# Two-block kernel on one core: modulation pieces taken out of the expert stages, and other instruction orders where stages meet

## The chip, the cores and the metric

One Trainium2 chip, one of its cores. The metric is the device time of one execution in microseconds; lower is better. The kernel was executed three times for the median, and once more under the profiler. Engines: TensorE (PE), VectorE (DVE), ScalarE (ACT), GpSimd (POOL) and SyncE (SP), which here only issues DMAs. Each engine works through its own list of instructions in order and waits on semaphores.

## The reference, cut to what matters

Batch 1, 256 tokens (two tiles of 128 rows), width 1024, everything float32.

```python
def first_block(x, ...):
    h = x
    for layer in range(2):
        h = h + hybrid_mixer(rms_norm(h, norm1_g[layer]), w_in[layer], ..., w_out[layer], lb)
        h = h + expert_choice_ffn(rms_norm(h, norm2_g[layer]), w_router[layer], w_gate[layer], w_up[layer], w_down[layer])
    return rms_norm(h, final_norm_g)

def expert_choice_ffn(xn, ...):            # 16 experts, 32 tokens each
    affinity = softmax(xn @ w_router)
    gate, idx = top_k(affinity.T, 32)      # each expert picks its tokens
    xe = xn[idx]
    ye = (silu(xe @ w_gate) * (xe @ w_up)) @ w_down * gate
    return scatter_add(ye, idx)

def second_block(x, c, ctx, c_ctx, ...):   # layer 0: pool mixer, layer 1: attention
    for i in range(2):
        sh1, sc1, gt1, sh2, sc2, gt2 = split(silu(c) @ w_ada[i] + b_ada[i], 6)
        csh1, ... = split(silu(c_ctx) @ w_ada[i] + b_ada[i], 6)
        x = x + gt1 * norm(mixer(modulate(norm(x), sh1, sc1)))
        x = x + gt2 * norm(mlp(modulate(norm(x), sh2, sc2)))
        # in layer 0 the same for ctx
```

The hybrid mixer projects to nine blocks of 512 columns, runs retention on four and HGRN2 on five, normalises both, multiplies by gates and applies w_out. The modulation vectors (w_ada: 2 layers x 1024 x 6144) depend on c alone, so they can be computed at any time before their use.

## The kernel before, in words

Time is a row of stages: layer 0 mixer, router, experts, layer 1 the same, then block 2 (pool mixer, MLP, attention, MLP). The context part of block 2 (its pool mixer and its MLP, nine pieces of weights in layer 0, nine in layer 1) is worked in between the experts.

**Weights and the ring.** All large weights come as pieces of 128 x 4096 float32 (2048 KB) into slots: four (0 to 3) of a ring of six, the last two of which (4, 5) hold w_high during mixers and MLPs, and two more (6, 7) in memory that the mixer has left. `item(name, slot, dmas)` writes down, at build time, in which slot a piece lies and how many pieces must be used before it may be loaded (`free_at`); PE counts used pieces in `weights_used`, and SP waits for that count ahead of each load (`load`, all loads at L2623). SP's list is in order, so a load that waits holds all behind it. Pieces of a mixer are sorted by `free_at`.

**Modulation pieces.** w_ada is cut into 12 pieces per layer. A piece is 8 matmuls (L537, 16 rows in a trace) into bank 6, ACT copies the row of 512 to `ada_s`, and four small matmuls (L552) turn it to columns, which PE can only do after ACT's copy. `ADA_EARLY`: six pieces per layer run in the mixer, between its projections. `ADA_LATE`: six per layer, one right after the output projection (`late_ada`), one after the logits, two after expert 0 and two after expert 1 (`LATE_AFTER`). `ada_bias` adds b_ada on DVE, `gains` makes the gains of the modulated norms.

**Split weights.** Mixer products are three passes over fp32r parts (L525, L526, L527): ACT copies a piece to w_high (`high_item`), DVE subtracts to get w_low (`low_item`). The activations are split likewise: `high_chunks` on ACT and `split_chunks` on DVE each write for every second bank a full xT and an xs_high (8 instructions each), and DVE subtracts both to xT_low (4 instructions).

**End of the mixer.** Order on ACT: last modulation row, `high_item(OUT_1)`, squares of the ret and hgrn outputs, sqrt of both (a table load ahead). On DVE: `low_item(OUT_0)`, sums, `low_item(OUT_1)`, then the hgrn rows (times 1/std), then gate x 1/std x ret rows, `ada_bias("early")`, `split_chunks`. PE: ret_out, hgrn_out, columns, transposes (L500), the output projection.

**Output projection and router.** Four products of 24 matmuls, tile 0 then tile 1, in banks 0 to 3; DVE adds each to h. Then a modulation piece, normalised rows xs of both tiles, 16 transposes, evacuation to xT with the gain, the logits of both tiles in one bank (L788), maximum, exp, affinity, a transpose of it (L796), four rounds of top-8 on DVE, spread (L802), gather (L815), expert 0 (L851 gate and up, L886 down).

**Block 2.** Attention's q, k, v weights are `mix2` items 0 to 2, w_o items 3 and 4, in a ring of four. PE: `turn_tile(0)` (L1211), projections (L1194), transposes of q (L1232) and k (L1239), scores (L1249).

ACT holds one set of function tables at a time; the program's first use of a function from another set is preceded by ACT_TABLE_LOAD.

## Time and profile before

| | us |
|---|---|
| median of 3 runs | 2110.59 |
| lowest, highest | 2109.51, 2112.42 |
| profiled execution, device time | 2113.23 |
| its span, first to last instruction | 2110.9 |
| PE busy in the span | 1744.7 (83%) |
| DVE, ACT, POOL busy | 796.9, 520.8, 36.4 |
| bytes by DMA | 629.10 MB, mean 298 GB/s |

All times of instructions are counted from the span's start. Busy shares are averages over stages of different kinds; the forty slices and the windows separate them. An instruction's row gives its start, how long it (or the merged group) took, engine, line, operation, output and inputs, and in brackets the engine's idle time before it and what ended it. Where a helper issues an instruction the line is the helper's (L425).

### The profile page before, as it was taken

To read this page: it belongs to the slowest core of one execution; us is meant where nothing else is said; L and a number is where in the kernel's file an instruction comes from. 1 tells how busy PE (TensorE), PEld (TensorE's weight loads), DVE (VectorE), ACT (ScalarE), POOL (GpSimd) and SP (SyncE) were. 2 spreads that over 40 slices of the span, in tenths; PEclk is the share of its full clock that TensorE was granted. 3 is DMA by queue.
4 is the path that set the end of the run, shared out by engine and by line. 5 is a ranking of instruction groups with operands and counts; after the bars stand their busy time and mean duration, and the time that the engine had idled before them with its cause. 6 is when DMAs were issued, how large, how long until landed. Compare 5 with 4: busy or idle time off the path is not lost.

```text
span 2110.9 us, 25989 instructions
## 1 busy us (share of the span) xinstructions
PE 1744.7 (83%) x10876; PEld 1150.9 (55%) x10876; DVE 796.9 (38%) x1175; ACT 520.8 (25%) x778; POOL 36.4 (2%) x42
## 2 busy tenths in 40 slices
PE   6998767678898849997677898866778999998998
PEld 5876423343454328875334354432247996457887
DVE  6594301211111026764201111121046676555766
ACT  5633110200000025432010000011144343343433
POOL 0000000000000000000000000000010000000000
PEclk9999778889999979998788999997889999998999
DMA  7475699999999993574899999999963454304451
GB/s 268 157 265 201 264 421 421 429 423 423 424 421 424 425 405 136 204 267 195 344 420 423 423 425 422 424 425 421 427 233 146 168 191 159 120 1 159 173 186 60
DMA packets 124799, 629.10 MB, mean 298 GB/s; under 512 B 5024, under 2 KB 7200, under 8 KB 99744
## 3 DMA queue, kind: packets, MB, share of 16 engines
q1 hardware_dynamic: 122000, 616.58, 72.9%
q0 software_dynamic: 2272, 9.44, 1.1%
q8 instruction: 73, 1.20, 0.2%
q10 hardware_dynamic: 432, 1.70, 0.2%
q14 instruction: 22, 0.18, 0.0%
HBM read 624.56 MB, written 3.15 MB: 297 GB/s over the span
## 4 chain that ended last, share of the span: by engine, by line
PE 57%; DMA 32%; DVE 5%; ACT 4%; issue 1%; SPq 0%; POOL 0%; DVEq 0%; ACTq 0%
DMA ring<-in_w_up 18%; PE bank L525 9%; PE bank L527 9%; PE bank L526 9%; PE bank L851 7%; DMA ring<-in_w_mlp_in 6%; PE bank L981 5%; PE bank L999 4%; DMA ring<-in_w_mlp_out 4%; PE bank L1194 2%; PE bank L537 2%; DMA ring<-in_w_in 1%; DVE w_low L425 1%; PE bank L1294 1%; ACT w_high L425 1%
## 5 line engine op out<-in xcount | busy, mean ns | idle before, releaser
L851 PE MATMUL bank<-ring,xeT 128*32 128x512 f32 x1984 | 285.2, 724 | 131.8 <-DMA ring<-in_w_up 131.5
L851 PEld LDWEIGHTS bank<-ring,xeT 128*32 128x32 f32 x1984 | 73.1, 124 | 333.1 <-issue 333.0
L425 ACT ACTIVATE silu_g<-bank 128x256 f32<-128x256 f32 x32 | 12.3, 384 | 741.7 <-PE bank L851 741.7
L425 DVE TENSOR_TENSOR hid_e<-silu_g,bank 128x256 f32<-128x256 f32 x32 | 13.5, 421 | 411.7 <-ACT silu_g L425 411.7
L525 PE MATMUL bank<-x_high,w_high 128*128 128x256 f32 x512 | 147.5, 288 | 11.0 <-DVE x_low L425 5.9
L2308 DVE TENSOR_TENSOR w_low<-ring,w_high 128x1024 fp32r<-128x1024 f32 x128 | 151.9, 1219 | 9.3 <-POOL y L425 4.9
L886 PE MATMUL bank<-ring,hid_T 128*32 128x256 f32 x2048 | 124.9, 390 | 29.9 <-DMA ring<-in_w_down 23.6
L981 PE MATMUL bank<-ctx_xT,ring 128*128 128x256 f32 x512 | 128.1, 417 | 25.7 <-DMA ring<-in_w_mlp_in 25.7
L1657 ACT ACTIVATE w_high<-ring 128x1024 fp32r<-128x1024 f32 x128 | 128.0, 1050 | 86.0 <-PE bank L527 86.0
L527 PE MATMUL bank<-x_high,w_low 128*128 128x256 f32 x512 | 146.4, 286 | 0.0
L526 PE MATMUL bank<-x_low,w_high 128*128 128x256 f32 x512 | 146.3, 286 | 0.0
L999 PE MATMUL bank<-ring,ctx_hid 128*128 128x512 f32 x256 | 122.4, 640 | 23.9 <-DMA ring<-in_w_mlp_out 23.9
L981 PEld LDWEIGHTS bank<-ctx_xT,ring 128*128 128x128 f32 x512 | 107.6, 212 | 47.7 <-DMA ring<-in_w_mlp_in 30.4
L525 PE MATMUL bank<-w_high,xs_high 128*128 128x512 f32 x256 | 106.9, 418 | 18.4 <-DVE xT_low L425 14.9
L425 DVE TENSOR_TENSOR w_low<-ring,w_high 128x2048 fp32r<-128x2048 f32 x44 | 100.8, 2292 | 25.1 <-ACT w_high L425 20.6
L886 PEld LDWEIGHTS bank<-ring,hid_T 128*32 128x32 f32 x2048 | 62.1, 111 | 82.6 <-DMA ring<-in_w_down 33.5
L525 PEld LDWEIGHTS bank<-x_high,w_high 128*128 128x128 f32 x512 | 98.6, 192 | 11.8 <-issue 11.6
L526 PE MATMUL bank<-w_low,xs_high 128*128 128x512 f32 x256 | 104.3, 407 | 0.0
L527 PE MATMUL bank<-w_high,xT_low 128*128 128x512 f32 x256 | 104.0, 406 | 0.0
L999 PEld LDWEIGHTS bank<-ring,ctx_hid 128*128 128x128 f32 x256 | 51.9, 206 | 91.6 <-issue 63.8
L527 PE MATMUL bank<-w_high,hid_low 128*128 128x512 f32 x256 | 101.5, 396 | 0.0
L525 PE MATMUL bank<-w_high,hid_high 128*128 128x512 f32 x256 | 101.5, 396 | 0.0
(275 smaller groups left out, 2630.9 us busy)
## 6 DMA issues: line engine op xcount, KB each, us to landing
ring<-in_w_down SPq DMA_DIRECT2D x64, 2048.0 KB, 25.5
ring<-in_w_gate SPq DMA_DIRECT2D x62, 2048.0 KB, 20.1
ring<-in_w_up SPq DMA_DIRECT2D x62, 2048.0 KB, 22.9
ring<-in_w_ada SPq DMA_DIRECT2D x24, 2048.0 KB, 9.9
ring<-in_w_mlp_in SPq DMA_DIRECT2D x24, 2048.0 KB, 8.6
ring<-in_w_mlp_out SPq DMA_DIRECT2D x24, 2048.0 KB, 7.9
ring<-in_w_in SPq DMA_DIRECT2D x18, 2048.0 KB, 9.1
ring<-in_w_out SPq DMA_DIRECT2D x4, 2048.0 KB, 8.1
```

The costliest lines, as they stand in the source:

```text
L425: self.ins, self.mine = op(*args, **kw), "none"
L525: mm(ps, lh, rh, start=first, stop=False, skip_group_check=True)
L526: mm(ps, lh, rl, start=False, stop=False, skip_group_check=True)
L527: return mm(ps, ll, rh, start=False, stop=last, skip_group_check=True)
L537: ins = mm(ps[32 * g:32 * g + 32, :], cT[:, 2 * g + k, :], w[:, 2 * g + k, :], start=k == 0, stop=k == 1)
L851: ins = mm(ps[32 * j:32 * j + 32, :], xeT[:, g % 2, c, i * CAP:(i + 1) * CAP], w[:, :, k, j, :, :], start=c == 0, stop=c == KC - 1, skip_g ...
L886: ins = mm(banks[q // 2][rows_, at_:at_ + 256], hidT[:, j, 32 * block:32 * block + 32], w[:, c, 256 * q:256 * (q + 1)], start=(n, c) == (0 ...
L981: ins = mm(ps[:, (j % 2) * S:(j % 2 + 1) * S], w[:, c, j * P:(j + 1) * P], cxT[:, c, :], start=c == 0, stop=c == KC - 1)
L999: ins = mm(ps[:, :], chid[:, c, t * P:(t + 1) * P], w[:, c, half * 512:(half + 1) * 512], start=c == 0, stop=c == 3)
L1194: ins = mm(ps[:, :], xT2[:, c, t * P:(t + 1) * P], w[:, c, :], start=c == 0, stop=c == KC - 1)
L1657: raw(w_high[:, n % 2, quarter(q)], ring[:, slot, quarter(q)], ACT.Copy).then_inc(S_("w_high_ready"), 1)
L2308: nc.vector.tensor_tensor(w_low[:, slot, quarter(q)], ring[:, slot, quarter(q)], w_high[:, n % 2, quarter(q)].bitcast(F32), ALU.subtract). ...
```

## The change

Three sorts of edits, in words:

1. Modulation pieces. The tables `EARLY_AFTER`, `ADA_LATE`, `LATE_AFTER`, `MOE_SLOTS` go. `ADA_EARLY` (six per mixer, at the same places), `ADA_REST` (four per layer, at the mixer's end and in the router) and `ADA_LAST` (four in block 2's attention) take their place; layer 1's mixer computes the last two pieces of layer 0 first. None is left among the experts. The slots of expert pieces rotate over 6, 7 once and then 4, 5, c, a, b, d.
2. The joints. Mixer end: squares and roots ahead of `high_item(OUT_1)`, `low_item(OUT_1)` behind `split_chunks`, sqrt tables loaded early by a one-column activation (`root_table`), ret rows multiplied by the gate first and by 1/std in place later; xs_high written by ACT from the banks for all chunks, xT_low made by DVE in one instruction from the bank. Router: h itself is transposed, 1/rms goes in as the scale of the exp; transposes and logits of tile 0 run inside the products of tile 1; banks 0 and 1 are used twice.
3. The start of a mixer: the first piece comes in two halves with their own semaphore, constants other than the identity and the masks are issued by SP behind it.

The diff, cut to its core (the signature changes of helpers are left out):

```diff
+ADA_EARLY = (pieces(0, 0, 6), pieces(0, 10, 12) + pieces(1, 0, 4))
+ADA_REST = (pieces(0, 6, 10), pieces(1, 4, 6) + pieces(1, 10, 12))
+ADA_LAST = pieces(1, 6, 10)
-LATE_AFTER = [{0: late[2:4], 1: late[4:6]} for late in ADA_LATE]
-MOE_SLOTS = (6, 7, 4, 5, 0, 1, 2, 3)
...
+        for piece, slot in zip(ADA_REST[layer], (b, d)):
+            item(("ada", *piece), slot, 1)
         for n in range(2):
             item(("w_out", layer, n), (c, a)[n], 1)
         count[2][4:6] = [count[0]] * 2
-        for n, slot in zip(ADA_LATE[layer][0:2], (b, d)):
-            item(("late", layer, n), slot, 1)
-        slots = itertools.chain(MOE_SLOTS, itertools.cycle(MOE_SLOTS[2:]))
+        for piece, slot in zip(ADA_REST[layer][2:], (b, d)):
+            item(("ada", *piece), slot, 1)
+        slots = itertools.chain((6, 7), itertools.cycle((4, 5, c, a, b, d)))
```

PE, end of the mixer, output projection and router:

```diff
             ret_out()
+            early_columns(len(ADA_EARLY[l]) - 1)
             hgrn_out()
-            early_columns(ADA_EARLY[l][-1])
             transposes(("mix", l), lambda t: xs[:, t, :], mix_ready)
+            rest_ada(0)
...
+            amid = {(0, 1): lambda: turn_rows(0), (1, 1): lambda: logits(0)}
             for t in range(NT):
                 for n in range(2):
...
                         fill(ins, name)
-            late_ada(ADA_LATE[l][0])
-            transposes(("x2", l), lambda t: xs[:, t, :], xs_ready)
+                        rest_columns(n)
+                        if n == 0:
+                            rest_ada(1)
+            turn_rows(1)
+            rest_ada(2)
+            logits(1)
+            rest_columns(2)
             pe.wait_ge(S_("affinity_ready"), NT * (l + 1))
...
+            rest_ada(3)
+            rest_columns(3)
```

PE, block 2:

```diff
+        ada_item(ADA_LAST[0], 1)
         turn_tile(0)
...
+                if (t, n) == (0, 0):
+                    last_columns(0, 1)
...
+        ada_item(ADA_LAST[1], 6)
         pe.wait_ge(S_("q_rot_ready"), NT)
...
+        last_columns(1, 6)
+        ada_item(ADA_LAST[2], 5)
         pe.wait_ge(S_("k_rot_ready"), NT)
...
+        last_columns(2, 5)
+        ada_item(ADA_LAST[3], 6)
...
         scores(1)
+        last_columns(3, 6)
```

ACT:

```diff
+                if (j, half) == (0, 0):
+                    act.wait_ge(S_("first_landed"), 16 * (l + 1))
...
-        act.dma_start(ident_all[:, :], consts).then_inc(S_("consts"), 16)
-        act.dma_start(AD[:, :, :].rearrange("p a b -> p (a b)")[:, 0:len(LEVELS) * P],
-                      masks).then_inc(S_("masks"), 16)
+        act.dma_start(ident_all[:, 0:P], consts[:, 0:P]).then_inc(S_("consts"), 16)
...
-                ins = f(logit[:, t, :], ps[:, t * NEXP:(t + 1) * NEXP], ACT.Exp,
-                        bias=rstats[:, t, 1:2], accum_out=rstats[:, t, 2:3])
...
+                free(f(logit[:, t, :], ps[:, 0:NEXP], ACT.Exp, scale=rinv[:, t:t + 1],
...
+                if e == NEXP - 1:
+                    root_table()
```

DVE:

```diff
+                    ins = stt(xT_low[:, c, :].rearrange("p (t n) -> p t n", t=NT),
+                              ps[:, at_:at_ + S].rearrange("p (t n) -> p t n", t=NT), gain(c),
+                              xs_high[:, :, c, :].bitcast(F32), ALU.mult, ALU.subtract)
...
             split_chunks(("mix", l), mix_gain)
+            low_item(OUT_1)
```

SP:

```diff
+                if name == ("mix", l, 0):
+                    sp.dma_start(whole[:, 0:4, :], halves[0]).then_inc(S_("first_landed"), 16)
+                    sp.dma_start(whole[:, 4:8, :], halves[1]).then_inc(landed[items[name][0]], 16)
+                if name == ("mix", 0, 0):
+                    sp.dma_start(ident_all[:, P:], consts[:, P:]).then_inc(S_("tables"), 16)
...
+                        if (e, n) == (0, 1):
+                            for piece in ADA_REST[l][2:]:
+                                early(("ada", *piece))
```

SP's list around expert 0 of layer 0, before. `ring_extra` are slots 6 and 7, a gate and an up row are the two halves of one half of an expert's gate and up weights.

```order
L2623 DMA ring_extra<-in_w_gate 128x4096
L2623 DMA ring_extra<-in_w_up 128x4096
L2623 DMA ring<-in_w_gate 128x4096
L2623 DMA ring<-in_w_up 128x4096
L2623 DMA ring<-in_w_down 128x4096 x2
L2623 DMA ring<-in_w_ada 128x8x512 x2
L2623 DMA ring<-in_w_gate 128x4096
L2623 DMA ring<-in_w_up 128x4096
L2623 DMA ring<-in_w_gate 128x4096
L2623 DMA ring<-in_w_up 128x4096
L2623 DMA ring<-in_w_down 128x4096 x2
L2623 DMA ring<-in_w_ada 128x8x512 x2
```

And of the change, from the same place:

```order
L2706 DMA ring_extra<-in_w_gate 128x4096
L2706 DMA ring_extra<-in_w_up 128x4096
L2706 DMA ring<-in_w_ada 128x8x512 x2
L2706 DMA ring<-in_w_gate 128x4096
L2706 DMA ring<-in_w_up 128x4096
L2706 DMA ring<-in_w_down 128x4096 x2
L2706 DMA ring<-in_w_gate 128x4096
L2706 DMA ring<-in_w_up 128x4096
L2706 DMA ring<-in_w_gate 128x4096
L2706 DMA ring<-in_w_up 128x4096
L2706 DMA ring<-in_w_down 128x4096 x2
```

The two pieces that stood behind expert 0 stand ahead of its ring loads, and the two behind expert 1 are gone.

PE's list from the last product of the output projection to the spread, layer 0, before:

```order
L527 MATMUL bank<-w_high,xT_low 128x512
L537 MATMUL bank<-ring,silu_c 32x512 x8
L500 MATMUL bank<-consts_sb,xs 128x128 x16
L788 MATMUL bank<-router_sb,xT 128x16 x16
L552 MATMUL bank<-consts_sb,ada_rows 128x2 x4
L537 MATMUL bank<-ring,silu_c 32x512 x8
L796 MATMUL bank<-consts_sb,affinity 16x128 x2
L802 MATMUL bank<-spread,ones 128x512 x2
```

And of the change:

```order
L528 MATMUL bank<-w_high,xT_low 128x512
L777 MATMUL bank<-consts_sb,h 128x128 x8
L539 MATMUL bank<-ring,silu_c 32x512 x8
L790 MATMUL bank<-router_sb,xT 128x16 x8
L554 MATMUL bank<-consts_sb,ada_rows 128x2 x4
L819 MATMUL bank<-consts_sb,affinity 16x128 x2
L539 MATMUL bank<-ring,silu_c 32x512 x8
L554 MATMUL bank<-consts_sb,ada_rows 128x2 x4
L827 MATMUL bank<-spread,ones 128x512 x2
```

Half of the transposes and logits have moved ahead into the projection, the transposes read h, and the second modulation piece stands behind the transpose of the affinity.

ACT's list at the end of layer 0's mixer, before:

```order
L425 ACTIVATE hgrn_off<-bank 128x512 x2
L425 ACTIVATE ada_rows<-bank 128x512
L425 ACTIVATE w_high<-ring 128x2048 x2
L425 ACTIVATE square<-bank 128x512 x2
L425 ACTIVATE xs,ssq<-bank 128x512 x2
L425 ACT_TABLE_LOAD
```

And of the change:

```order
L434 ACTIVATE hgrn_off<-bank 128x512 x2
L434 ACT_TABLE_LOAD
L434 ACTIVATE spare<-eps 128x1
L434 ACTIVATE ada_rows<-bank 128x512
L434 ACTIVATE square<-bank 128x512 x2
L434 ACTIVATE kdec,ssq<-bank 128x512
L434 ACTIVATE std<-ssq,eps 128x1
L434 ACTIVATE ret_stat<-ret_stat,eps 128x8
L434 ACTIVATE kdec,ssq<-bank 128x512
L434 ACTIVATE std<-ssq,eps 128x1
L434 ACTIVATE w_high<-ring 128x2048 x2
```

The table load stands ahead of the squares, and the conversion of the piece (w_high) behind both roots.

## Rows read from the trace of the kernel before

**Rows 1.** The page's part 2: GB/s in 40 equal slices of the span.

```profile
GB/s 268 157 265 201 264 421 421 429 423 423 424 421 424 425 405 136 204 267 195 344 420 423 423 425 422 424 425 421 427 233 146 168 191 159 120 1 159 173 186 60
```

**Rows 2.** Windows: us; busy PE, PEld, DVE, ACT, POOL; clock, DMA, GB/s.

```profile
300.00:500.00 200.00, 139.16 (x1071) 70.22 (x1070) 28.13 (x46) 29.02 (x49) 2.64 (x3) 0.86 1.01 424
...
1070.00:1300.00 230.00, 185.29 (x1228) 98.60 (x1232) 27.58 (x46) 16.81 (x31) 0.00 (x0) 0.90 1.01 424
```

**Rows 3.** Timeline of SP: loads around expert 0 and expert 1, layer 0.

```profile
219.75 16.72 SPq L2623 DMA_DIRECT2D ring<-in_w_ada  x2
262.01 0.34 SPq L2623 DMA_DIRECT2D ring<-in_w_gate  x1
...
284.20 8.69 SPq L2623 DMA_DIRECT2D ring<-in_w_ada  x2
```

**Rows 4.** Timeline, layer 0: end of the mixer, output projection, router, expert 0.

```profile
169.00 0.95 PE L552 MATMUL bank<-consts_sb,ada_rows 128*128 128x2 f32 x8
...
169.88 1.92 PE L537 MATMUL bank<-ring,silu_c 128*32 128x512 f32 x16
...
178.74 4.69 DVE L425 TENSOR_TENSOR w_low<-ring,w_high 128x2048 fp32r<-128x2048 f32 x2
...
179.89 1.28 ACT L425 ACT_TABLE_LOAD   x1
...
187.72 1.54 PE L500 MATMUL bank<-consts_sb,xs 128*128 128x128 f32 x6 [7.78 <-DVE xs L425]
...
193.57 0.47 PE L525 MATMUL bank<-w_high,xs_high 128*128 128x512 f32 x1 [1.96 <-issue]
...
217.86 0.69 DVE L425 TENSOR_TENSOR h<-h,bank 128x512 f32<-128x512 f32 x1 [4.93 <-PE bank L527]
...
232.78 3.25 PE L537 MATMUL bank<-ring,silu_c 128*32 128x512 f32 x16
...
236.38 0.41 DVE L425 COPY affinityT<-bank 16x256 f32<-16x256 f32 x1 [2.35 <-PE bank L796]
...
254.42 3.89 PE L851 MATMUL bank<-ring_extra,xeT 128*32 128x512 f32 x32 [0.94 <-issue]
```

**Rows 5.** A window at the mixer's end, layer 0, columns as in rows 2.

```profile
185.00:188.00 3.00, 0.28 (x2) 0.29 (x3) 2.58 (x5) 0.00 (x0) 0.00 (x0) 0.50 1.04 440
```

**Rows 6.** Timeline, layer 1: last sum, logits, first product of expert 0.

```profile
987.12 0.69 DVE L425 TENSOR_TENSOR h<-h,bank 128x512 f32<-128x512 f32 x1 [4.93 <-PE bank L527]
...
993.91 4.46 PE L788 MATMUL bank<-router_sb,xT 128*128 128x16 f32 x32 [2.02 <-ACT xT L425]
...
1022.22 2.04 PE L851 MATMUL bank<-ring_extra,xeT 128*32 128x512 f32 x16 [0.94 <-issue]
```

**Rows 7.** Timeline: the start of the program.

```profile
15.58 3.85 ACT L425 ACTIVATE w_high<-ring 128x2048 fp32r<-128x2048 f32 x2 [3.37 <-DMA ring<-in_w_in]
...
22.77 0.80 PE L525 MATMUL bank<-w_high,xs_high 128*128 128x512 f32 x1 [7.28 <-DVE xT_low L425]
...
28.84 0.50 PE L525 MATMUL bank<-w_high,xs_high 128*128 128x512 f32 x1 [0.97 <-DVE xT_low L425]
```

**Rows 8.** Timeline: the start of layer 1's mixer.

```profile
780.52 1.28 ACT L425 ACT_TABLE_LOAD   x1
781.82 0.29 ACT L425 ACTIVATE std<-ssq,eps 128x1 f32<-128x1 f32 x1
...
791.71 0.76 PE L525 MATMUL bank<-w_high,xs_high 128*128 128x512 f32 x1 [5.25 <-DVE xT_low L425]
...
797.73 0.51 PE L525 MATMUL bank<-w_high,xs_high 128*128 128x512 f32 x1 [1.35 <-DVE xT_low L425]
```

**Rows 9.** Timeline of PE in block 2: first transposes, q transposes, first scores.

```profile
1778.61 1.06 PE L1211 MATMUL bank<-consts_sb,xs 128*128 128x128 f32 x8 [2.00 <-issue]
...
1827.74 1.97 PE L1232 MATMUL bank<-consts_sb,q_rot 128*128 128x128 f32 x16 [1.94 <-DVE q_rot L425]
...
1832.85 3.65 PE L1249 MATMUL bank<-kT,qT 128*128 128x512 f32 x4 [0.98 <-DVE kT L425]
```

409 lines of the change are left out of this document (227 added, 182 removed).

## Prediction, made before the change was run

> **What bounds the kernel now.** I read the page's forty slices first, then the windows, and only then the order of time at the places where one stage meets the next. The reader is to see two kinds of stretch [rows 1]: long runs of slices at 420 to 429 GB/s, and slices at 136 to 268 GB/s. The first are the two expert stages, the others the mixers and block 2. The windows say it sharper [rows 2]: over 200 us in layer 0 and 230 us in layer 1 the DMA engines are busy at a share of 1.01 and move 424 GB/s, while PE is busy 139 of 200 us and 185 of 230 us. There a piece of weights (2048 KB = 2.097 MB) costs 2.097/0.424 = 4.95 us, whoever uses it, and no engine's work costs anything as long as slots come free in time. Between these stages the DMA has nothing to do for long, and what counts is the chain PE, ACT, DVE at each joint: mixer to output projection, output projection to router to expert 0, last expert to next stage.
>
> **1. Pieces out of the saturated stretch.** Before, a layer loads four modulation pieces in its expert stage. Two are issued at 219.75, ahead of the stretch, and two at 284.20, in it; the saturated stretch begins at 262.01, when expert 0 has used its second pair and expert 1's first load goes out [rows 3]. After, the two later ones are gone, and the slots in which the two earlier ones lay are free by the router, so that expert 1's first two pieces load there, in the gap ahead of the stretch. So four pieces fewer are left when the stretch begins: 4 x 4.95 = 19.8 us, twice: **39.6 us**. Condition: these two loads, in SP's order behind the four of expert 0, are in by the restart. Six pieces take 29.7 us from the end of the output projection, and the restart comes some 34 us after it (part 2), so yes, with 4 us to spare. The later pieces are used in block 2, where the DMA idles. Bounds: 19.8 us in all if the two preloads never come early, 41 if the stretch's other traffic shrinks with it.
>
> **2. Router joint, layer 0.** Now [rows 4]: the last hgrn output leaves PE by 180; ACT has converted w_out 1 ahead of the squares, a table load stands at 179.89, DVE converts for 4.69 us from 178.74, and only then come the normalised rows; PE transposes at 187.72 after 7.78 us of idle, and multiplies from 193.57. After, both conversions come behind the statistics, the sqrt table is loaded early, the ret rows are multiplied before the sqrt is known, and high and low parts are made without a full copy (8 instructions each on ACT and DVE in place of 8 on ACT and 12 on DVE, about 0.5 us each). Step by step with the same durations: hgrn output 179.9 (columns now ahead of it, +0.9), last rows 183.4, transposes to 184.5, first low part 187.1. But PE has modulation piece 0 to run there: 1.92 us at the full clock, 3.25 at the half [rows 4]. After the idle the granted clock is 0.50 of 2.4 GHz, that is 1.2 GHz [rows 5], and 2.6 us of idle remain; I take the low clock, and PE is ready at 188.8, **4.8 us** earlier (bounds 3 and 6.5).
>
> Into the output projection go, all on PE and on the path: two sets of columns (0.95 each), a piece (1.92), eight transposes (about 1.1, half of the sixteen at a joint) and the logits of tile 0 (half of 4.46 [rows 6], a bit less at full clock: 1.8), in sum **+6.7 us**. The other side: from the last sum at 217.86 to the copy of the affinities at 236.38 it is 18.5 us now, through normalise, transposes, the logits of both tiles, table load, exp, and a PE that runs a piece of 3.25 us at 232.78 ahead of the transpose which is on the path [rows 4]. After, per step: sum 0.7, eight transposes to 1.9, ACT statistics and four evacuations to 4.3 (a piece on PE hides in it), logits of one tile to 6.4, maximum and exp to 7.5, affinity to 8.4, copy at 8.65: **-10.0 us** (bounds 8 and 11). The search of the top 32 and the gather are as before, and the last piece with its columns (1.92 + 0.95, or some 5 at the low clock) lies beside the 6.9 us of the search; its cover would have to shrink by 2 us before it cost anything. Net 4.8 - 6.7 + 10.0 = **8 us** (bounds 4 and 11). The first expert started at 254.42, now about 246.4.
>
> **3. Router joint, layer 1.** The same, but from 987.12 to expert 0 at 1022.22 it is 35.1 us, not the 36.6 of layer 0 [rows 4, 6]: 1.5 us less to win, and the earlier half I put 0.5 lower. **6 us** (bounds 3 and 9).
>
> **4. The start.** PE's first product is at 22.77, behind the conversion at 15.58, which waited for its weights [rows 7]; by then x, weights, constants, masks and columns have come, 4.85 MB by their shapes, 12.1 us at 0.4 MB/us and 3.4 us for the rest. After, constants and masks stand behind the weights: x, 1.25 MB with columns and identity, by about 6 (3.1 + 3.4 is 6.5; ACT began at 6.6 before), the second half of the weights, 3.3 MB, at 11.7. Then two statistics without table loads 3.2, to 9.2; two conversions of 1.93, the second from 11.7, to 13.6; high parts 1.0, low parts 1.1: 15.8. That is 7.0, and the 0.97 us that PE waited at 28.84 for the next low part go too: **8 us** (bounds 2, if only copies and table loads go, and 9.5). The next item's weights land about 21 and are wanted by PE at 29.5.
>
> **5. Layer 1's start.** A table load (1.28) at 780.52, then a short wait for the weights, PE's first product at 791.71, and a stall of 1.35 us at 797.73 [rows 8]. After, the first piece takes the slot that expert 15's first pair frees, one piece earlier in SP's order; ACT may convert from 782.8, high and low to 788.8: 2.8 us, and the stall goes: **4.1 us** (bounds 1.3 and 4.1). The table load ahead of block 2 goes too, **1.3 us**.
>
> Here a rule speaks for more. What the row shows: the load takes 1.28 us and std begins at 781.82, at its end [rows 8]. The Trainium skill (ScalarE: Activation LUTs, What ACT_TABLE_LOAD costs) puts a drain of about 1.38 us behind each switch, 2.66 us in all. Eight switches leave the path (two at the start, two in each router joint, one ahead of layer 1's mixer, one ahead of block 2). By the page the sum would be 11 us larger, by the row it stands.
>
> **6. Block 2 pays.** Four pieces and four sets of columns come to PE's order. Piece 0 fits the 2.00 us ahead of 1778.61; its columns wait for ACT's copy: +1.4 in a stretch where PE is busy throughout. Piece 1 (1.92) fits the 1.94 us ahead of 1827.74. Pieces 2 and 3 stand between the q transposes and the scores at 1832.85, where PE idled 2.5 us and two times 2.87 come, with two waits for ACT's copy of the row behind its four copies of q: scores +3.35; the last columns +0.5; the four scores took 3.65 us at the low clock and gain 1 [rows 9]. In sum **+4 us** (bounds 0 and 8). Who waits: DVE's and ACT's softmax, directly. The kv weights are now issued when the MLP ends, alone on the queue, 4.95 us of bytes and wanted some 14 us later. The output weights load later too, about 40 us before use.
>
> **Sum.** 39.6 + 8 + 6 + 8 + 4.1 + 1.3 - 4 = 63 us. The profiled execution took 2113.23 with a span of 2110.9; it would take 2050.2, span 2047.9. The median of the runs is 2110.59, 2.64 under the profiled one: 2110.6 - 63 = **2047.6 us**.
>
> **Rivals.**
> *A, the sum as it stands:* 2047.6, own range 2037 to 2058.
> *B, the preload fails:* expert 1's pieces are held by pieces 2 and 3 of the modulation (PE reaches the last at about 10 us after the output projection; held past the restart it would be two pieces a layer). For: SP works in order. Against: 4 us to spare. 2047.6 + 19.8 = 2067.
> *C, joints gain little:* the clock stays at 1.2 GHz through the output projection, and the start is bound by its bytes. Router joints 3 us each worse, start 6 (its lower bound), block 2 at its upper bound 4: 16, that is 2064.
> *D, joints gain more:* PE's filled gaps hold 2.4 GHz through the joints, the gather too (matmuls that now run at the low clock): 3 for each of two gathers, 2.5 each for the output projections, 1 for block 2: 12, so 2036.
> *E, slower:* the ring. A load waits until all items but the last few are used. In the item tables of the code 12 expert-stage loads are issued with four or fewer pieces between them and the last release that they need; after the change it is 25, and two have three. If each of the 25 left the DMA idle for more than 63/25 = 2.5 us, nothing would be left; at a full piece, 4.95 us each, it is 2047.6 + 124 = 2171. Against it: the 12 of now show no slice below 420 GB/s in the stage [rows 1], and three pieces are 15 us of queue.
> *F, dearer table loads:* each load that is gone had held ACT as long again as its row shows (1.28 us); eight times that is 10 us more, 2037. Against it: at 781.82 the next instruction begins at the load's end. This mechanism is the one of the Trainium skill above.
> That the change does nothing of the kind I exclude: SP's rows show no modulation load behind expert 0.
>
> **Chances.** A 0.55, C 0.18, D 0.13, B 0.10, F 0.02, E 0.02. The likeliest is A: 2047.6. For eight in ten I reach to D and F below, 2034, and past C to 2065; B and E stay outside, and some of the tails. Same means within 0.2%, about what runs of this kernel tell from no change (their own spread is 0.14%): faster 0.97, same 0.01, slower 0.02, the last from E.
>
> **What would show it.** (1) The expert stages stay at 424 GB/s and are 19.8 us shorter from the first DMA of the stretch to the last expert's product; an idle of some us at a share under 1 within them is E. (2) From the last sum of the output projection to expert 0: 26.7 us. If it is over 30, the piece ahead of the logits or the last columns are on the path. (3) First product at about 15 us; at 20 the bytes bound it. (4) Two expert 1 loads land before the restart; else B. (5) The scores begin 4 to 5 us later, counted from the MLP's end. The prediction is wrong above all if (1) fails, which holds two thirds of it.

## The result and the profile after

| | before | after |
|---|---|---|
| median, us | 2110.05 (4 runs) | 2031.20 (4 runs) |
| lowest, highest | 2104.61, 2112.42 | 2030.25, 2033.38 |
| span of the profiled execution | 2110.9 | 2029.1 |

The ratio is 0.9631, 95% interval 0.9611 to 0.9651: 79 us faster. The forecast was 63 (2047.6, range 2034 to 2065), so the direction was right and the size too small, and 2031.2 lies 3 us under the range. Between the two spans there are 81.8 us; the profiled execution of before (2113.23) was 3.2 us above the median of this table.

Page of after, part 2, GB/s in 40 slices. The saturated runs are at the rate of [rows 1]; a slice is 50.7 us now and was 52.8.

```profile
GB/s 303 170 247 290 376 428 423 428 420 424 422 425 419 427 312 166 242 290 284 414 422 425 422 423 420 424 427 423 415 134 171 202 169 162 249 34 133 203 169 62
```

Both traces, cut at the same instructions (starts of TensorE's first products, ends of VectorE's last sums), beside what the prediction's terms give for each piece:

| from, to | before | after | gain | forecast |
|---|---|---|---|---|
| start, first product | 22.77 | 15.82 | 7.0 | 7.0 |
| to the last sum of the output projection, layer 0 | 195.78 | 190.82 | **5.0** | -0.9 |
| to expert 0 | 35.87 | 25.41 | 10.5 | 10.0 |
| to the last expert's last sum | 526.77 | 509.80 | 17.0 | 19.8 |
| to layer 1's first product | 10.52 | 7.80 | 2.7 | 2.8 |
| to the last sum of the output projection, layer 1 | 196.10 | 190.70 | **5.4** | -1.1 |
| to expert 0 | 34.41 | 25.48 | 8.9 | 8.5 |
| to the last expert's last sum | 529.29 | 509.11 | 20.2 | 19.8 |
| to the first product of block 2's first MLP | 40.43 | 36.29 | **4.1** | 1.3 |
| to the q projection | 189.91 | 188.05 | **1.9** | 0 |
| to the scores | 51.00 | 55.07 | -4.1 | -4.8 |
| to the first product of the second MLP | 86.14 | 85.35 | 0.8 | 0.5 |
| to the end, less its last 3 us (alike in both) | 188.85 | 186.36 | **2.5** | 0 |
| sum | | | 81.8 | 63 |

So the terms for pieces, bytes and instructions hold, to 0.5 us mostly and to 2.8 in one case. The 18.8 us too few are in three places that I had at about nothing or at 1.3: the mixers with their ends (12.3), block 2's start (2.8) and its two MLPs (4.4). The experiments are about these.

These are two executions, and some stretches come out differently from one execution of the same instructions to the next. From expert 0 of layer 0 to the last sum the unedited changed kernel took 509.80, 505.81 and 510.04 us in its three profiles; from the last sum of the projection to expert 0 the kernels with the old order took 34.4 to 34.5 or 35.9 to 36.1, in either layer. By this alone a row's gain can be 2 to 4 us off.

Timeline of after. It answers to [rows 3, 4, 7 and 8]: the first product, last sum, transpose of the affinities, expert 0; two more loads of SP (209.79, 218.28) ahead of the restart at 239.66; the last expert of layer 0 and layer 1's first product.

```profile
15.82 0.80 PE L526 MATMUL bank<-w_high,xs_high 128*128 128x512 f32 x1 [3.32 <-DVE xT_low L434]
...
205.95 0.69 DVE L434 TENSOR_TENSOR h<-h,bank 128x512 f32<-128x512 f32 x1 [2.47 <-PE bank L528]
...
209.79 0.33 SPq L2706 DMA_DIRECT2D ring<-in_w_gate  x1
...
214.05 0.59 PE L819 MATMUL bank<-consts_sb,affinity 128*16 128x128 f32 x2 [0.20 <-DVE affinity L434]
...
218.28 0.33 SPq L2706 DMA_DIRECT2D ring<-in_w_up  x1
...
232.05 3.87 PE L878 MATMUL bank<-ring_extra,xeT 128*32 128x512 f32 x32 [0.94 <-issue]
...
239.66 0.33 SPq L2706 DMA_DIRECT2D ring<-in_w_gate  x1
...
728.84 1.28 ACT L434 ACT_TABLE_LOAD   x1
...
730.42 0.38 ACT L434 ACTIVATE hid_T<-bank 128x256 f32<-128x256 f32 x1
...
730.86 5.35 PE L913 MATMUL bank<-ring,hid_T 128*32 128x256 f32 x64 [1.03 <-ACT hid_T L434]
...
749.65 0.76 PE L526 MATMUL bank<-w_high,xs_high 128*128 128x512 f32 x1 [3.48 <-DVE xT_low L434]
```

Windows of after: the output projection, and expert 0 up to the restart (columns as in rows 2), and after them the projection of before.

```profile
176.93:206.64 29.71, 28.98 (x156) 22.96 (x152) 13.02 (x20) 5.57 (x13) 0.70 (x1) 1.00 0.51 195
232.05:239.66 7.61, 7.54 (x64) 2.23 (x64) 3.23 (x9) 0.00 (x0) 1.28 (x2) 1.00 0.85 325
```

```profile
193.57:218.55 24.98, 24.98 (x104) 19.42 (x108) 6.76 (x11) 2.99 (x7) 0.70 (x1) 0.93 0.01 3
```

The reader is to see two things. The projection of before ran at a mean granted clock of 0.93, that of after at 1.00 throughout, with 6.7 us of work put into it and only 4.7 us more time. Products of the projection of before, at the full clock first and about a microsecond later at 1.2 GHz:

```profile
193.88 0.39 PE L526 MATMUL bank<-w_low,xs_high 128*128 128x512 f32 x1
...
195.00 0.63 PE L527 MATMUL bank<-w_high,xT_low 128*128 128x512 f32 x1
```

That projection has twelve products in its first 4 us (mean granted clock 0.62) and is at the full clock again from 197.98. And the DMA was idle for 0.15 of 7.61 us, 1.1 us, ahead of the restart. The second preload (issued at 218.28) landed at 238.83, 0.8 us ahead of the restart at 239.66 and not 4. The router has no load there, and the context's loads are issued at 236.27 and later, behind it; the six pieces landed 32.2 us after the last sum where the forecast had 29.7, in part since the first took 7.2 us from issue to landing, and the restart came 33.0 us after that sum for the 34.

### The profile page after: what moved, and what is told of

Same layout as the page of the kernel before. It is cut to its first block, busy times and chain, and to the rows that moved or that the text cites. A ratio compares the mean times of both kernels' runs of the same rounds, so it can differ in the third digit from the quotient of the medians.

```text
span 2029.1 us, 26064 instructions
## 1 busy us (share of the span) xinstructions
PE 1705.6 (84%) x10876; PEld 1130.6 (56%) x10876; DVE 789.6 (39%) x1179; ACT 523.6 (26%) x794; POOL 37.4 (2%) x42
## 4 chain that ended last, share of the span: by engine, by line
PE 59%; DMA 27%; issue 5%; ACT 4%; DVE 3%; POOL 0%; SPq 0%; ACTq 0%; DVEq 0%; POOLq 0%
DMA ring<-in_w_up 14%; PE bank L526 9%; PE bank L528 9%; PE bank L527 9%; PE bank L878 7%; DMA ring<-in_w_mlp_in 6%; PE bank L1026 5%; DMA ring<-in_w_mlp_out 5%; PE bank L1008 5%; PE bank L1217 2%; PE bank L539 2%; PE bank L1329 1%; PE bank L682 1%; ACT w_high L434 1%; DMA ring<-in_w_ada 1%
## 5 line engine op out<-in xcount | busy, mean ns | idle before, releaser
L878 PE MATMUL bank<-ring,xeT 128*32 128x512 f32 x1984 | 278.9, 710 | 142.3 <-DMA ring<-in_w_up 142.0
L434 ACT ACTIVATE silu_g<-bank 128x256 f32<-128x256 f32 x32 | 12.3, 383 | 741.8 <-PE bank L878 741.8
L1008 PE MATMUL bank<-ctx_xT,ring 128*128 128x256 f32 x512 | 120.5, 399 | 26.0 <-DMA ring<-in_w_mlp_in 26.0
L1008 PEld LDWEIGHTS bank<-ctx_xT,ring 128*128 128x128 f32 x512 | 102.1, 201 | 45.4 <-DMA ring<-in_w_mlp_in 30.3
```

Source lines behind the costliest of these rows:

```text
L434: self.ins, self.mine = op(*args, **kw), "none"
L878: ins = mm(ps[32 * j:32 * j + 32, :], xeT[:, g % 2, c, i * CAP:(i + 1) * CAP], w[:, :, k, j, :, :], start=c == 0, stop=c == KC - 1, skip_g ...
L1008: ins = mm(ps[:, (j % 2) * S:(j % 2 + 1) * S], w[:, c, j * P:(j + 1) * P], cxT[:, c, :], start=c == 0, stop=c == KC - 1)
```

## Experiments

Each kernel ran with runs of the kernel before beside it on its chip. The changed kernel itself, unedited, was the yardstick of two batches: 2027.61 (ratio 0.9618, interval 0.9605 to 0.9631) and 2032.41 (0.9642, 0.9629 to 0.9655). A ratio has some 0.0013 to either side, 2.8 us; 0.001 is 2.1 us. But the changed kernel stands at 0.9618, 0.9642 and 0.9631 in three batches, 5 us apart at most, so a difference under 5 us can be told only between kernels of one batch, or in the traces. The batches are: a_same, a_no_root, a_hold_pair, a_no_amid (0.9618); a_again, a_best, a_gap, a_last_out (0.9642); the others have no unedited changed kernel beside them.

> The changed kernel itself, unedited, so that what is run beside it is compared on one chip and the ratio to the kernel before has more runs behind it. 2031 us, ratio 0.962 to 0.964.

> The changed kernel, unedited, once more, as the yardstick of the three beside it. Ratio 0.961 to 0.963.

### The bytes of the saturated stretch

```diff
+        for n in range(2):
+            free_at[("moe", layer, 1, n)] = free_at[("moe", layer, 1, 2)]
```

> The changed kernel, but expert 1's first two pieces may load only when the third may, at the restart of the queue behind expert 0, so that the gap ahead of it stays empty as before the change. Theory: two pieces a layer move back into the saturated stretch, 4 times 4.95 us: 19.8 us, 2051. Rival (the stretch has slack that takes them up, and the gain came from the joints): under 10 us, 2031 to 2041.

Measured 2048.18, ratio 0.9711, against 0.9618 of the changed kernel on the same chip: 20.6 us. In the trace expert 0 to expert 3's sum takes 10.0 us longer in layer 0 (136.22 for 126.20) and 10.4 in layer 1.

```diff
+                if (e, n) in ((4, 0), (6, 0)):
+                    item(("pad", layer, e), next(slots), 1)
```

> The changed kernel with two more loads of 2048 KB in each expert stage, one in expert 4 and one in expert 6, of weights that nothing reads (TensorE only waits for them). Theory: the stretch is bound by bytes, each piece costs 4.95 us: four times that, 19.8 us, 2051. Rival (a piece can hide, or costs more by the slot it takes from the ring's look-ahead): under 10 us, 2041 or less, or over 30 us.

Measured 2048.52, ratio 0.9718: 21 us by the ratio of 0.9618, 16 by 0.9642, so 4.0 to 5.2 us for each of the four pieces. Bytes are the bound, the ring has look-ahead enough, and rival E has nothing to stand on: with the restart as origin the last expert's last pair of products comes 501.94 us later before (262.01 to 763.95) and 482.13 after (239.66 to 721.79), a difference of 19.81 for the forecast 19.8; in layer 1 504.12 and 484.17, 19.95. What layer 0 lost of it lies behind that pair, in the last expert.

### The table loads

In the changed kernel the early sqrt load falls into the last expert ahead of a copy that TensorE waits for (728.84 and 730.42 above).

```diff
-                if e == NEXP - 1:
-                    root_table()
...
                         free(f(hidT[:, :, :], ...
+                        if e == NEXP - 1:
+                            root_table()
```

> The changed kernel with the last expert's early sqrt table load placed behind the copy of the transposed hidden rows in place of ahead of it. In the changed kernel that copy waited for the load (0.55 us), and in layer 0 the down products behind it ran in 5.35 us in place of 3.87 us. Theory: 0.55 us twice, and another 1.1 us in layer 0 if the short wait is what lowered the clock there: 1.1 to 2.2 us, 2029 to 2030. Rival: the load now delays the copy of the last expert's rows or nothing changes: 2031.

Measured 2026.61, ratio 0.9614 (0.9601 to 0.9628), without a yardstick in its batch. The copy comes 0.55 us earlier in both layers; the time can't be told from the changed kernel's. The low clock of the down products isn't this load's: in the profile of a_same the copy waits the same 0.55 us, and the products behind it take 3.73 us and not 5.35.

```diff
         def root_table():
-            step(f(spare[:, :], eps[:, :], ACT.Sqrt))
+            pass
```

> The changed kernel without its early one-column sqrt activations: the sqrt tables are loaded where a root first needs them, at the start, at both mixers' ends (two), after both last experts (two). Theory (a load costs its own row, 1.28 us): 5 times 1.28 us, less what the early load cost in the last experts (0.55 us twice, up to 1.1 us more in layer 0), so 4 to 5.3 us: 2035 to 2036. Rival (each load holds the engine as long again): 5 times 2.66 us less the same: 2042 to 2043. A third: the loads are hidden by other waits: 2031.

Measured 2040.34, ratio 0.9678: 12.7 us slower than the changed kernel on the same chip. Of three expectations the middle one (12) has the sum, but not its reason, and it counted five loads where six came onto the path. Timeline of this kernel at block 2's start, ScalarE and TensorE:

```profile
1477.73 1.28 ACT L434 ACT_TABLE_LOAD   x1
...
1479.03 0.29 ACT L434 ACTIVATE std<-ssq,eps 128x1 f32<-128x1 f32 x1
...
1487.73 10.05 PE L1183 MATMUL bank<-band_sb,xs 128*128 128x256 f32 x32 [3.06 <-DVE xs L434]
```

The same place in the profile of the changed kernel, TensorE:

```profile
1482.42 7.14 PE L1183 MATMUL bank<-band_sb,xs 128*128 128x256 f32 x32
...
1491.44 7.14 PE L1198 MATMUL bank<-ring,diffT 128*128 128x256 f32 x32 [1.87 <-DVE diffT L434]
```

std begins at the load's end, so the load holds ScalarE for its own 1.28 us and no more. But TensorE, which waits for what comes behind, idles 3.06 us, and its granted clock falls: the pooling products take 10.05 us and not 7.14. From the last sum to the MLP it is 40.44 for 36.29 us, 4.15 for one load of 1.28 (36.0 to 36.9 us in ten other profiles without that load and without dummies). At the mixer's end of layer 0 it is 2.8 us for one load against a_same (12.19 and 6.16 for 10.91 and 4.68), with the transposes at 3.65 and the modulation piece at 2.65 us for 2.26 and 1.92, and 2.3 against the profile of after, whose transposes were slow too (3.38); the two at the start cost 2.3 in all, since the second conversion no longer waits for its weights. (The Trainium skill, ScalarE: Activation LUTs, What ACT_TABLE_LOAD costs, gives 2.66 us a switch with a drain behind the load. Six loads here cost 2.1 us each on average, near it, but no row shows a drain of ScalarE; at block 2's start the rest is TensorE's clock, and for the other loads the rows above show it in part.)

### TensorE's clock at the joints

```diff
+        def warm(bank, n):
+            if frees[bank]:
+                pe.wait_ge(bank_free[bank], frees[bank])
+            for _ in range(n):
+                mm(psum[bank][:, :], ident, ident_all[:, 0:512], start=True, stop=True)
...
+            warm(4, 7)
             transposes(("mix", l), lambda t: xs[:, t, :], mix_ready)
```

> The kernel before, with seven dummy products (identity times 512 constant columns) on TensorE ahead of the transposes at each mixer's end, where it idled 7.78 and 7.40 us. Theory (clock): most of what the router joints gave beyond the forecast came from TensorE no longer idling long, so that the granted clock stays at 2.4 GHz: the sixteen transposes shrink from 3.6 to about 2.2 us and the output projection from 24.98 to 23.3 us (96 products at 0.232 us and the tail), in sum 3 us a layer, 6 us: 2104. Rival (placement): the projection gained because of the order of the work in it; dummies change nothing or delay the transposes: 2110 to 2112.

Measured 2110.18, ratio 1.0007 (0.9996 to 1.0018): nothing. The trace of this kernel tells why. In layer 0 the dummies kept the clock up for the transposes, but 2.26 us of idle were left behind them, and the projection began at 1.2 GHz (window of 192 to 194: clock 0.50). In layer 1 the last ten transposes ran at the low clock already (2.40 us for the 1.31 below), with the dummies ahead of them. Layer 0:

```profile
188.77 1.31 PE L506 MATMUL bank<-consts_sb,xs 128*128 128x128 f32 x10 [0.96 <-DVE mods L425]
...
192.34 0.77 PE L531 MATMUL bank<-w_high,xs_high 128*128 128x512 f32 x1 [2.26 <-issue]
```

```profile
192.00:194.00 2.00, 1.66 (x4) 1.41 (x5) 1.75 (x4) 1.66 (x4) 0.00 (x0) 0.50 0.00 0
```

So two more dummies into that gap, behind the transposes:

```diff
+            warm(4, 7)
             transposes(("mix", l), lambda t: xs[:, t, :], mix_ready)
+            warm(0, 2)
```

> The kernel before with seven dummy products ahead of the transposes at each mixer's end and two more between the transposes and the output projection, where b_warm still idled 2.26 us and the projection began at 1.2 GHz. Theory (an idle of about 2 us just ahead of it is what lowers the clock of the projection): it begins at 2.4 GHz and takes 23.3 us in place of 24.98, 1.7 us a layer and some of the transposes: 2106 to 2107. Rival (the clock falls whatever stands there): 2110.

Measured 2104.98, ratio 0.9987 (0.9977 to 0.9996). The projection's first product, of this kernel:

```profile
191.55 0.47 PE L531 MATMUL bank<-w_high,xs_high 128*128 128x512 f32 x1 [0.53 <-issue]
```

That is 2.7 us (0.8 to 4.9 by the interval), the smallest difference here whose interval leaves 1 out. The projection takes 24.30 us for b_warm's 26.06 in layer 0 and 24.30 for 24.71 in layer 1. Against the kernel before it is only 0.7 and 0.5, less than the 1.7 expected. The granted clock is 1.00 throughout, and at the full clock TensorE now reaches the second low parts before VectorE has them:

```profile
195.18 0.50 PE L531 MATMUL bank<-w_high,xs_high 128*128 128x512 f32 x1 [0.59 <-DVE xT_low L425]
```

The old low parts, made in a further four instructions from two full copies, were the next wait; the changed kernel makes each in one from the bank. That the clock pays more there is what a_gap, below, tests.

```diff
+                if n == 3:
+                    warm(6, 2)
...
+        warm(0, 3)
         post_rows("rows_mix0", 0)
         pe.wait_ge(S_("bands_landed"), 16)
+        warm(4, 3)
```

> As b_warm, and in addition two dummies ahead of the fourth modulation piece of each mixer (TensorE waited 2.57 us for its load and then ran it in 3.22 us where others take 1.92), three ahead of the gate rows and three ahead of the pooling products at block 2's start (idle 3.22 and 3.07 us, then 3.78 and 10.04 us of products that take 1.96 and 7.14 us at the full clock). Theory (clock): 1.3 us for each of two pieces and up to 4.7 us in block 2, so about 7 us less than b_warm, 2097. Rival: as b_warm, 2110.

Measured 2106.82, ratio 0.9994 (0.9985 to 1.0003). Block 2's start shrank from 40.40 to 37.05 us, as far as the theory says. The modulation piece ran in 1.92 us, but layer 1's router took 1.7 us longer than in b_warm (36.04 for 34.38), at a place that the edit doesn't touch, and of the 7 us expected under b_warm some 3 came: the sum is under what the runs resolve. The term itself, of before and of after:

```profile
140.69 3.22 PE L537 MATMUL bank<-ring,silu_c 128*32 128x512 f32 x16 [2.57 <-DMA ring<-in_w_ada]
```

```profile
131.20 1.92 PE L539 MATMUL bank<-ring,silu_c 128*32 128x512 f32 x16 [1.40 <-DMA ring<-in_w_ada]
```

The piece came 1.2 us earlier and ran 1.3 us shorter. It is not a fixed price, nor the old order's alone: in b_warm the same idle of 1.39 us was followed by the low clock, after the change 1.40 was not. In all profiles without dummies at this place the piece was slow (2.4 to 3.6 us) in 4 of 8 mixers with the old order and in 7 of 28 with the new; the waits ahead of it were 1.3 to 2.8 us where it was slow and 0.6 to 2.0 where it was not.

The reverse in the changed kernel: the piece between transposes and projection cut to almost nothing.

```diff
-            for k in range(2):
+            for k in range(0 if piece in (ADA_REST[0][0], ADA_REST[1][0]) else 2):
...
+            if piece in (ADA_REST[0][0], ADA_REST[1][0]):
+                ins = mm(ps[0:32, 0:64], cT[:, 0, :], w[:, 0, 0:64], start=True, stop=True)
```

> The changed kernel with the first modulation piece of each mixer's end cut to one product of 64 columns (part of the modulation vectors is left out), so that TensorE idles some 2.5 us between the transposes and the output projection, where the piece ran. Theory (the piece was no cost but kept the granted clock at 2.4 GHz): the projection begins at 1.2 GHz and takes 1.7 us longer in each layer, 3.4 us more than the changed kernel. Rival (the piece only cost time): equal or up to 1 us less.

Measured 2031.64, ratio 0.9640, the changed kernel beside it 0.9642: equal. In layer 1 the idle came (2.21 us) and the clock fell a microsecond into the projection, whose products go from 0.39 to 0.63 us:

```profile
908.65 0.47 PE L526 MATMUL bank<-w_high,xs_high 128*128 128x512 f32 x1 [2.21 <-issue]
...
909.65 0.40 PE L527 MATMUL bank<-w_low,xs_high 128*128 128x512 f32 x1
909.88 0.54 PE L528 MATMUL bank<-w_high,xT_low 128*128 128x512 f32 x1
910.21 0.63 PE L526 MATMUL bank<-w_high,xs_high 128*128 128x512 f32 x1
```

It took 31.28 us for 29.76, and began 0.5 us sooner after the transposes. In layer 0 the transposes themselves ran at the low clock (3.41 us for 2.26), so that less idle was left, and nothing fell (29.69). So the piece is free where it stands, and where it keeps the clock up that is worth 1.5 us; one layer of two shows it, and the time as a whole doesn't.

Nor is 2.60 us of idle a sure sign of what follows. Ahead of the transposes at the mixers' ends the changed kernel idles 2.60 us in 24 mixers of twelve profiles, with the same products ahead of it and the same sixteen transposes behind: they took 2.26 us, at the full clock, in 8 of them, and 3.2 to 3.6 in 16.

```diff
+            warm(4, 2)
             transposes(("mix", l), ...
...
+        warm(0, 4)
         post_rows("rows_mix0", 0)
...
         transposes("xm0", ..., first=4)
+        warm(0, 5)
```

(and three dummies at layer 1's mixer start, four ahead of the second MLP)

> The changed kernel with dummy products where TensorE still idles: two ahead of the transposes at the mixers' ends, three at the start of layer 1's mixer, four ahead of block 2's first gate rows, five and four ahead of the two MLPs of block 2. Theory (clock): 0.8 us at each mixer's end (ScalarE's conversion bounds it), 2 to 2.5 at layer 1's start, 1 at the gate rows, 2 to 2.5 at each MLP: 9 us, 2022. Rival: the granted clock at a stage's start follows something else than the idle ahead of it: 2031, or more where the dummies run late.

Measured 2026.14, ratio 0.9621 (0.9607 to 0.9634), which can't be told from the changed kernel where 9 us were expected. In its trace the dummies at the MLPs win 2 us each (first product to q projection 185.88 for 188.3 and 187.9 of the unedited kernel, last stretch 184.50 for 186.5 and 186.3). At the gate rows they ran late and cost 2. At layer 1's start the clock was up and nothing to speak of was won; windows of this kernel from its first product:

```profile
745.75:747.75 2.00, 2.00 (x10) 1.65 (x10) 1.83 (x3) 1.81 (x4) 0.00 (x0) 1.00 0.78 291
747.75:749.75 2.00, 1.03 (x5) 0.51 (x3) 1.87 (x2) 1.89 (x2) 0.00 (x0) 1.00 0.49 190
749.75:751.75 2.00, 1.38 (x6) 1.15 (x7) 1.69 (x5) 1.91 (x2) 0.00 (x0) 1.00 0.13 48
```

PE is busy 1.03 and 1.38 of 2 us at the full clock, while DVE and ACT are busy throughout: it waits for the low parts. A higher clock pays only where TensorE is the one that others wait for.

### Placement in the router

```diff
-                                     amid.get((n, t), lambda: None))
+                                     lambda: None)
...
+            turn_rows(0)
             turn_rows(1)
             rest_ada(2)
+            logits(0)
             logits(1)
```

(with VectorE's router work of tile 0 moved behind the projection too)

> The changed kernel with the transposes and the logits of tile 0 behind the output projection in place of inside it. The projection gets 2.9 us shorter (1.05 and 1.85 us), and from its last sum to the spread it takes longer by those two and by ScalarE's and VectorE's evacuation and statistics of tile 0. Theory: 3 to 4 us a layer, 6 to 8 us in all, 2037 to 2039; the inner placement carries about half of the router joint's gain. Rival: the gain of the router came from transposing h itself and the roots out of the path, not from the placement: within 1 us a layer, 2031 to 2033.

Measured 2027.64, ratio 0.9617, the changed kernel 0.9618: nothing. The projection is 2.7 us shorter (27.02 for 29.74), the way from its last sum to the spread 1.8 longer (16.70 for 14.89) and to expert 0 another 0.5. The inner placement, the most intricate of the joint's edits, gains nothing. With everything behind the projection it is still 27.7 us from the last sum to expert 0 in both layers, 8.2 and 6.7 less than before. That comes from the rest: h transposed ahead of its statistics, 1/rms in the exp, tables loaded early, the piece behind the affinities. How much each of these gives no run shows.

### The start

```diff
+                if (l, j) == (0, 0):
+                    act.wait_ge(S_("first_landed"), 16)
+                    act.wait_ge(landed[slot], value)
...
+        act.dma_start(ident_all[:, P:], consts[:, P:]).then_inc(S_("tables"), 16)
+        act.dma_start(AD[:, :, :].rearrange("p a b -> p (a b)")[:, 0:len(LEVELS) * P],
+                      masks).then_inc(S_("masks"), 16)
```

> The changed kernel with the program's start as before in its transfers: the other constants and the masks are issued by ScalarE's queue at the start, and the first conversion waits for both halves of the first piece. Theory: 3.3 MB ahead of the first conversion become the 4.85 MB of before, so it starts some 4 us later: first product at 19 to 20 us, 2034 to 2035. Rival (the bytes were not what bound the start, the table loads and copies were): 2031 to 2032.

Measured 2036.46, ratio 0.9655, against 0.9618 and 0.9642: 3 to 8 us. The first product is at 21.84 for 15.9, and the stretch from there to ret_out another 1 to 3 longer. Of the start's 7 us the order of the transfers carries 6, and copies and table loads 0.9 (22.77 to 21.84); I had named the lower bound 2 for the case that only these were left, twice too much.

### Block 2

```diff
-                for g in range(4):
+                for g in range(1 if piece in ADA_LAST else 4):
```

> The changed kernel with the four modulation pieces of block 2 multiplied on a quarter of their rows only (part of the modulation vectors is left out), so that each is 0.5 us on TensorE and not 1.92; loads, copies and columns stay. Theory: pieces 2 and 3 stand on the path ahead of the scores, 1.44 us each, the other two in idle time: 2.9 us less, 2028. Rival (they are hidden, or the clock falls where they were): 2031.

Measured 2029.08, ratio 0.9622: equal to the changed kernel. But the edit took no time off the piece; two of its eight products last as long as all of them (row of this kernel, beside 1.92 us and 16 rows in [rows 4]):

```profile
1743.81 1.90 PE L539 MATMUL bank<-ring,silu_c 128*32 128x512 f32 x4
```

Products into four different groups of 32 rows of a bank run side by side. (The Trainium skill, TensorE: Matmul & The Clock Gate, Part 3: Packing small matmuls, says the same of products at different places of the array.) So once more, with the pieces nearly gone:

```diff
-            for k in range(2):
+            for k in range(0 if piece in ADA_LAST else 2):
...
+            if piece in ADA_LAST:
+                ins = mm(ps[0:32, 0:64], cT[:, 0, :], w[:, 0, 0:64], start=True, stop=True)
```

> The changed kernel with the four modulation pieces of block 2 cut to one product of 64 columns each (part of the modulation vectors is left out). Theory (block 2 pays for pieces 2 and 3 on the path): 1.85 us for each, 3 to 4 us less than the changed kernel. Rival (TensorE idles there and its clock falls, or it waits for the rotated q and k anyway): within 1 us of it.

Measured 2031.63, ratio 0.9640 for 0.9642. From q projection to scores it takes 53.05 us for 55.07, so 2.0 of the 4.1 us that block 2 pays are the pieces' products. The other 2.05 are their columns and the waits that stand in the products' place (rows of this kernel), not told apart, and the waits are why not 3.7 came back. The time as a whole is unchanged; of the 2.0 us the last stretch took back 0.9 in this profile:

```profile
1747.49 1.97 PE L1264 MATMUL bank<-consts_sb,q_rot 128*128 128x128 f32 x16 [1.71 <-DVE q_rot L434]
...
1752.56 1.02 PE L556 MATMUL bank<-consts_sb,ada_rows 128*128 128x2 f32 x8 [0.96 <-ACT ada_rows L434]
```

### The MLPs, whose code the change leaves alone

In the MLPs a product of 256 columns follows the one before after 120.0 ns in the kernel before and its three variants with dummies, in all 32 stretches of 91 products that I read, and after 118.7 ns in most stretches of the changed kernel and its variants, after 120.0 in the others. Start of a product and of the 90th behind it, before, (1707.74 - 1696.94)/90 = 120.0 ns, and after, (1625.77 - 1615.09)/90 = 118.7 ns. The change adds one tile, spare, and all tiles placed behind it lie 32 bytes further.

```diff
     eps = place("eps", [P, 1])
+    spare = place("spare", [P, 1])
```

> The kernel before with the changed kernel's one new tile (spare, one column) placed where the changed kernel places it, unused, so that all tiles behind it lie 32 bytes further. Question: in both MLPs of block 2 a product of 256 columns follows the one before after 120.0 ns in all four executions of the kernel before and its variants with dummies, and after 118.7 ns in most passes of the changed kernel, with the same instructions; that is 1.9 and 2.4 us of its gain. If the tiles' addresses do it: 118.7 ns here, 4 us less, 2105. If not (the instruction stream or something dynamic): 120.0 ns, 2109.

Measured 2106.47, ratio 0.9978 (0.9964 to 0.9992). The last stretch takes 186.33 us, as after (186.36) and not as before (188.85), the first MLP's 188.52 for 189.91, and 118.7 ns stand in seven of eight stretches, with the kernel before's instructions. So one unused column goes with 3.9 us in the two stretches and 4.6 in the ratio, whose interval reaches from 1.7 to 7.6 us and which is no larger than the distance between batches; the trace is the better witness. Nor is all of the 3.9 the pace. The first 10 us of the second MLP, before and in b_spare:

```profile
1918.99:1928.99 10.00, 10.00 (x61) 10.00 (x62) 4.23 (x7) 2.54 (x4) 1.49 (x1) 0.69 0.00 0
```

```profile
1915.83:1925.83 10.00, 10.00 (x70) 10.00 (x71) 5.30 (x9) 3.61 (x5) 1.48 (x1) 0.82 0.00 0
```

Nine products more at 120 ns are 1.1 us of the 2.5, by the granted clock (0.69 and 0.82). In the first MLP it was the same in both (0.73 and 0.72), and there 1.4 us came. So the pace alone is worth some 1.4 us a MLP, 2.8 of the measured 79. Whether the column moves that too isn't shown: the clock of these 10 us is 0.69 or 0.70 in all four profiles without the column and 0.69 to 0.86 in those of the changed kernel and its variants without dummies there.

### What beats both

The changed kernel with the sqrt load behind the last expert's copy, dummies ahead of both MLPs (five and four) and three at layer 1's start:

```diff
+        transposes("xm0", ..., first=4)
+        warm(0, 5)
...
+        transposes("xm1", ..., first=0)
+        warm(6, 4)
```

> The changed kernel with what the runs so far found: the last expert's sqrt table load behind the copy of the hidden rows, and dummy products ahead of both MLPs of block 2 (five and four) and at layer 1's mixer start (three), but none at the gate rows, where four of them ran late in a_warm and cost about 2 us. Theory: 2.0 and 2.4 us at the MLPs, 0.55 us twice in the last experts, nothing at layer 1's start, where TensorE then waits for VectorE: 5 to 6 us under the changed kernel on the same chip. Rival (what the dummies win is given back by the clock later): within 2 us of it.

Measured 2023.86 us, ratio 0.9603 (0.9590 to 0.9616), against 2032.41 and 0.9642 of the changed kernel on the same chip: 8 us under it (5 to 6 were expected), 84 under the kernel before. Its parts are not shown: the one profile is of its slowest run (2029.31), and there the last MLP won 1.8 us, but the first hardly any (187.40 us for 187.94 of the unedited kernel; the clock fell behind the dummies, 0.83 in its first 10 us).

## Why the prediction was off, point by point

The mechanism that holds two thirds of the sum, bytes taken out of the saturated stretch, was right. What failed is the sizing of the joints: the stretches from a mixer's first product to the last sum of its output projection were put at -0.9 and -1.1 us and gave 5.0 and 5.4. Besides, a table load was priced by its own row alone (1.3 for 4.1), and the MLPs were put at nothing (4.4).

- **Part 1, 39.6 us: held.** Measured 37.2 with the tails, and 39.8 from the restart to the last pair. Two experiments price four pieces at 20.6 and at 16 to 21 us. What is missing is layer 0's last expert. The new table load there stands ahead of a copy on the path (0.55 us, my omission), and the last pair and the down products ran at the low clock for longer (6.58 and 5.35 us, before 5.45 and 3.86). The second is the execution's and not the change's: in a_same they took 5.45 and 3.73, and the whole expert stage of layer 0 gave 21.0 us.
- **Parts 2 and 3, the router joints, 8 and 6: the term that was mis-sized.** With what belongs to them (stalls of the start taken off) they gave 14.5 and 13.0. From the last sum on the steps were right (10.5 and 8.9 for 10.0 and 8.5). Ahead of it, the "+6.7 us" put into the projection cost 4.7 and 5.0: the sum took the 24.98 us of before, with its 3.4 us at 1.2 GHz, as the work's price, and at the granted clock of 1.00 it is less. The clock is worth 0.7 and 0.5 us in the old order (b_warm_two) and 1.5 in the new one (a_gap, one layer). The earlier half gave 5.8 and 5.2 for 4.8 and 4.3, inside its bounds. And the stretch from the first product to ret_out, which I did not look at beyond the stall, gave 3.0 and 3.8 more. In layer 0's two profiles 1.2 of it are the wait for the fourth modulation piece and 1.3 that piece's low clock; the rest isn't placed. It varies: in layer 0 it is 146.6 to 149.0 us, mean 147.8, in the five profiled kernels with the old order (148.96 in the one of the table), and 143.5 to 147.7, mean 144.9, in thirteen with the new one (145.04). So 2.9 of the 3.9 us in the table are the change's, 0.97 of them the stall that I had counted. In layer 1 the means are 147.7 and 145.1, so 2.6 of the table's 5.1 are the change's, 1.35 of them the stall. What lies beyond is the luck of the two executions. So was part 3's "1.5 us less to win" in layer 1: b_spare has 36.1 us there, and b_warm_two 34.5 in layer 0. The copy was put at 8.65 us and 18.5 less that is 9.9, not 10.0.
- **Part 1's 4 us to spare: wrong,** 0.8. The pieces landed 2.5 us later than bytes alone have it, and the restart came a microsecond sooner. It held all the same.
- **Part 4, 8, part 5, 4.1: held,** 7.9 and 4.1.
- **Part 5's last load, 1.3: mis-sized,** 4.1. The row's 1.28 us were right and what it sets off was not in the sum: TensorE's idle and 2.9 us of low clock behind it.
- **Part 6, -4: held** up to the scores (-4.1), with 2.0 for the pieces' products and the rest for columns and waits.
- **The MLPs, 0: 4.4.** No reading of the diff's instructions could have given it; b_spare shows 3.9 of it with the tile's 32 bytes alone, some 2.8 by the pace of the products.

Rival D (2036, full clock through the joints) had the mechanism of part of the difference and 0.13 of the chances. Its projections came (2.0 and 1.7 for 2.5 each), its gathers hardly did (spread and gather 3.78 and 5.68 us for 3.77 and 6.45 in layer 0, for the 3 us less that it named), and it lacked block 2's start and the MLPs; that its sum is near the measured one is in part luck. Rival B was nearer than I had it (0.8 us to spare), and rival C did not come. Rival F is settled: no load holds ScalarE beyond its row, and still the loads put back on the path cost 2.1 us each on average, from 0.95 at layer 1's start (8.75 for 7.80) to 4.15 at block 2's.

What stays open: which of the router's edits give its 8.2 and 6.7 us, what of the 32 bytes matters to TensorE's pace, why a stretch of the same loop has 120.0 ns in one execution and 118.7 in another, and what decides whether an idle of 1.4 or of 2.60 us is followed by the low clock.

## What to carry to other kernels

Price a wait that you remove by what the waiting engine does behind it, too: on TensorE an idle of 2.60 us was followed by 1.2 GHz in 16 of 24 cases, so 1.28 us of table load cost up to 4.15. A low clock that the trace of before shows in a stretch is part of that stretch's price and can go if the idle goes, but it pays only where TensorE is what others wait for. And it can be the execution's: profile the same kernel twice before a stretch's 2 us are put down to a change. Small differences in stages that the change doesn't touch can come from where tiles lie; put the new tile into the old kernel alone before a story is told of them.

## What the runs showed of the hardware that I had not expected

- An unused tile that shifts the others by 32 bytes changes the pace of TensorE's products from 120.0 to 118.7 ns for 256 columns, some 1.4 us in each MLP of b_spare.
- Eight products into four groups of 32 rows of a bank took 1.92 us and two of them 1.90.
- A table load of 1.28 us costs 4.15 us at block 2's start, with std beginning at its end.
- Seven dummies, 6.25 us, in an idle of 7.8 won nothing while 2.26 us of idle were left behind them; with two more the kernel was 2.7 us faster than the one before.
- The same instructions behind the same 2.60 us of idle ran at 2.4 GHz in 8 mixers' ends and at 1.2 in 16.
